# Eight modulation chunks summed by GpSimd in place of VectorE, in a one-core two-block transformer kernel

## The reference

```python
mod = jax.nn.silu(c) @ w_ada[l] + b_ada[l]            # w_ada: 1024 x 6144
sh1, sc1, gt1, sh2, sc2, gt2 = jnp.split(mod[:, None, :], 6, axis=-1)
h = modulate(rmsnorm(x, g_norm1[l]), sh1, sc1)
cq, ckv, kpe, rq, rk, rv, rg = split_proj(h @ w_in[l])
...                                                   # latent attention and retention
x_new = x + gt1 * o
x_new = x_new + gt2 * conv_ffn(modulate(rmsnorm(x_new, g_norm2[l]), sh2, sc2), ...)
```

## Time and profile before

| | |
|---|---|
| median of 3 runs | 933.84 us (929.66 to 933.9) |
| profiled execution | 929.45 us, span of its instructions 927.6 us |
| TensorE busy | 850.9 us (92%) |
| VectorE busy | 600.5 us (65%) |
| ScalarE busy | 462.0 us (50%) |
| GpSimd busy | 15.7 us (2%) |
| granted TensorE clock, mean | 0.969 of full |

### The profile page before, as it was taken

The page is one execution under the profiler, slowest core; times in us unless marked ns, Lnnn a source line. Parts: engine busy times, 40 slices in busy tenths (PEclk is TensorE's granted clock), DMA queues, the critical chain, the costliest instruction groups (busy, mean ns, idle before and its releaser), DMA issues. The chain is left out here.

```text
span 927.6 us, 13571 instructions
## 1 busy us (share of the span) xinstructions
PE 850.9 (92%) x5330; PEld 751.0 (81%) x5330; DVE 600.5 (65%) x921; ACT 462.0 (50%) x720; POOL 15.7 (2%) x21
## 2 busy tenths in 40 slices
PE   4799798989999999999999999988989699999996
PEld 2598686857889999998788967677967599999885
DVE  4956987759667888885557667466544655555443
ACT  5736255154555666664445574545444454444441
POOL 1001000000000000000000000000000000000000
PEclk9989998999899999999999999989999799999998
DMA  9932685016556556555556542234514256555541
GB/s 340 341 140 69 198 289 204 23 56 215 184 160 205 182 182 182 183 182 193 172 158 248 182 140 96 69 101 149 179 49 139 78 184 184 185 185 183 182 159 45
DMA packets 103223, 152.91 MB, mean 165 GB/s; under 512 B 6474, under 2 KB 55670, under 8 KB 103160
## 3 DMA queue, kind: packets, MB, share of 16 engines
q1 hardware_dynamic: 101160, 146.00, 48.2%
q10 hardware_dynamic: 2000, 6.04, 1.7%
HBM read 150.97 MB, written 1.05 MB: 164 GB/s over the span
## 5 line engine op out<-in xcount | busy, mean ns | idle before, releaser
L1795 DVE TENSOR_TENSOR w_lo<-raw,w_hi 128x1024 fp32r<-128x1024 f32 (+1 forms) x244 | 294.5, 1214 | 206.8 <-ACT w_hi L1306 206.6
L1306 ACT ACTIVATE w_hi<-raw 128x1024 fp32r<-128x1024 f32 (+1 forms) x244 | 254.3, 1050 | 247.6 <-PE bank L691 114.5
L765 PE MATMUL bank<-hT_hi,w_hi 128*128 128x256 f32 x864 | 246.4, 285 | 7.9 <-DVE hT_lo L1856 6.7
L766 PE MATMUL bank<-hT_lo,w_hi 128*128 128x256 f32 x864 | 245.9, 285 | 0.0
L767 PE MATMUL bank<-hT_hi,w_lo 128*128 128x256 f32 x864 | 245.8, 285 | 0.0
L765 PEld LDWEIGHTS bank<-hT_hi,w_hi 128*128 128x128 f32 x864 | 167.2, 194 | 9.3 <-issue 8.0
L767 PEld LDWEIGHTS bank<-hT_hi,w_lo 128*128 128x128 f32 x864 | 167.3, 194 | 0.0
L766 PEld LDWEIGHTS bank<-hT_lo,w_hi 128*128 128x128 f32 x864 | 167.3, 194 | 0.0
L689 PE MATMUL bank<-w_hi,hT_hi 128*128 128x512 f32 (+2 forms) x224 | 90.7, 405 | 17.4 <-DVE w_lo L1795 9.9
L690 PE MATMUL bank<-w_lo,hT_hi 128*128 128x512 f32 (+2 forms) x224 | 88.4, 394 | 0.0
L691 PE MATMUL bank<-w_hi,hT_lo 128*128 128x512 f32 (+2 forms) x224 | 88.4, 394 | 0.0
(11 more groups left out here) (317 smaller groups left out, 1172.3 us busy)
## 6 DMA issues: line engine op xcount, KB each, us to landing
raw<-w_up_dram SPq DMA_DIRECT2D x132, 256.0 KB, 3.1
raw<-w_ada_dram SPq DMA_DIRECT2D x48, 512.0 KB, 4.9
raw<-w_down_dram SPq DMA_DIRECT2D x44, 512.0 KB, 3.3
raw<-w_in_dram SPq DMA_DIRECT2D x40, 512.0 KB, 4.6
raw<-w_gate_dram SPq DMA_DIRECT2D x44, 256.0 KB, 2.8
raw<-w_out_dram SPq DMA_DIRECT2D x16, 512.0 KB, 3.6
raw<-wk_x_dram SPq DMA_DIRECT2D x8, 512.0 KB, 4.0
raw<-wv_x_dram SPq DMA_DIRECT2D x8, 512.0 KB, 3.2
```

What stands on the lines that cost most here:

```text
L765: pe.matmul(o, hi[:, c:c + P], xh[:, k, :], start=f, stop=False, skip_group_check=True)
L766: pe.matmul(o, hi[:, c:c + P], xl[:, k, :], start=False, stop=False, skip_group_check=True)
L1306: act.activation(unit_view(w_hi[n % NSPLIT], u), unit_view(raw[u % NRAW], u), ACT.Copy).then_inc(w_hi_ready, 1)
L1795: dve.tensor_tensor(unit_view(w_lo[n % NSPLIT], u), unit_view(raw[u % NRAW], u), unit_view(w_hi[n % NSPLIT], u).bitcast(F32), ALU.subtract ...
```

## The change

The 64 row tiles of the sum units are handled by GpSimd. VectorE's one fused instruction becomes two on GpSimd, since the raw tile is first multiplied in place and then added: 64 multiplications and 64 additions (four of the latter are plain copies, for the first row tile of chunks 6 to 9). Ahead of each of them GpSimd waits for its own previous instruction (`settle`). `accumulate` is called from GpSimd's loop over the norms: s0 to s15 right after the power of norm "mem", s16 to s31 right after that of "ret". `unit_ready` now counts split units only, and a new semaphore `sum_ready` counts sum units; SyncE and TensorE wait for the one that fits. VectorE skips sum units, and its feed in the rounds of "mla" is gone.

```diff
@@ TensorE @@
-                    pe.wait_ge(unit_ready, u + 1)
+                    pe.wait_ge(unit_ready, split_of[u] + 1)
...
-                pe.wait_ge(unit_ready, last_unit[f"ada{p}"] + 1)
+                pe.wait_ge(sum_ready, sum_no[last_unit[f"ada{p}"]] + 1)
@@ SyncE @@
-                    sp.wait_ge(unit_ready, u - NRAW + 1)
+                    if summed[u - NRAW]:
+                        sp.wait_ge(sum_ready, sum_no[u - NRAW] + 1)
+                    else:
+                        sp.wait_ge(unit_ready, split_of[u - NRAW] + 1)
@@ GpSimd @@
+            def accumulate(u):
+                name, k0, nk, cols, _ = units[u]
+                chunk = int(name[3:])
+                acc = sum_of(chunk)
+                pool.wait_ge(raw_landed[u % NRAW], landed[u])
+                if k0:
+                    pool.wait_ge(sum_ready, sum_no[u])
+                for k in range(k0, k0 + nk):
+                    w = raw[u % NRAW][:, (k - k0) * cols:(k - k0 + 1) * cols]
+                    settle()
+                    step(pool.tensor_scalar(w, w, csilu[:, 0, k:k + 1], None, ALU.mult))
+                    settle()
+                    if k:
+                        ins = pool.tensor_tensor(acc, acc, w, ALU.add)
+                    elif chunk in SUMMED_EARLY:
+                        pool.wait_ge(in_gate, 32)
+                        ins = pool.tensor_tensor(acc, gate_of(chunk), w, ALU.add)
+                    else:
+                        if chunk in (6, 8):
+                            for p in SUMMED_EARLY[chunk - 6:chunk - 4]:
+                                ready(pool, ("spread", p))
+                        ins = pool.tensor_copy(acc, w)
+                    if k < k0 + nk - 1:
+                        step(ins)
+                ins.then_inc(sum_ready, 1)
...
                 pool.tensor_tensor(rstd[:, n, 0:w], var[:, n, 0:w], mhalf[:, 0:w], ALU.pow).then_inc(rstd_ready, 1)
+                if name in ("mem", "ret"):
+                    pool.wait_ge(csilu_ready, 2)
+                    for u in sum_units[16 * (name == "ret"):16 * (name == "ret") + 16]:
+                        accumulate(u)
@@ VectorE: accumulate() is removed @@
                     if summed[u]:
-                        if units[u][1]:
-                            dve.wait_ge(unit_ready, u)
-                        accumulate(u)
                         continue
...
-                    elif kind == "mla":
-                        feed_units(base_unit + n + 1)
```

More of the change, by code:

```diff
@@ L282, in build @@
     split_of = {u: n for n, u in enumerate(split_units)}
+    sum_units = [u for u in range(len(units)) if summed[u]]
+    sum_no = {u: n for n, u in enumerate(sum_units)}
     ends = set(last_unit.values())
@@ L462, in build @@
         unit_ready = sem("unit_ready")
+        sum_ready = sem("sum_ready")
+        pool_step = sem("pool_step")
         w_used = sem("w_used")
@@ L1270, in _, with step, settle @@
             pool.wait_ge(mhalf_ready, 1)
+            steps = [0]
+            def step(ins):
+                steps[0] += 1
+                ins.then_inc(pool_step, 1)
+            def settle():
+                pool.wait_ge(pool_step, steps[0])
+            def accumulate(u):
[23 more added lines that the diff above has]
+                ins.then_inc(sum_ready, 1)
             for n, name in enumerate(POWS):
@@ L1758, in feed @@
                 feed_units(reach(last_unit[name] + 1 if name else 0))
[L1760 to L1782, removed]
             def feed_units(stop):
```

## The result

The changed kernel takes 996.95 us (994.28 to 998.98) against 932.65 us of the kernel before, a ratio of 1.0694 (95% interval 1.0664 to 1.0723): 64 us slower, where 8.5 had been forecast and the range ended at 958, 25 us above the kernel before. The profiled execution has a span of 997.1 us against 927.6: these two lie 69.5 us apart, because the profiled execution of the changed kernel is the slowest of its four (998.98) and that of the kernel before (929.45) lies 3 us under its median. Differences of places in the two traces add up to 69.5, not to 64.

A forecast was written before the change was run, and what follows sets the result against it. VectorE was taken to bound 95.6 to 153.9 us and TensorE attention. The terms 6.4 + 1 + 2.1 - 1 gave +8.5 us, so 942.3 us for the median, with a range of 926 to 958.

The forecast's parts named there:

- 8.5 us of idle TensorE: 95.6 to 153.9 us: the most idle TensorE time that could be won there, 58.3 less 49.8.
- P: GpSimd's time per sum unit of two row tiles, each one product and one addition of 128x512: taken as 3.9 us.
- upper bound, 6.2: Dearest GpSimd time per sum unit: two and three passes with the power's larger fixed part, 6.2 us.
- (c): Rival: GpSimd itself bounds attention, 5.0 us a unit without turns; early stretch -1, attention +19.7, total +18, 952 us; chance 0.20.
- (d): Rival: slow GpSimd and turns both, 4.5 us a unit, 6.0 with turns; +12.8, +11.7 and +1, total +25, 959 us; chance 0.10.
- turns: GpSimd and VectorE instructions locking each other out of SBUF: 1.5 us a unit in full for s4 to s15, 1.3 taken.
- Stretch 1: 78.5 to 95.6 us: GpSimd's first sums beside a busy VectorE; 0 side by side, about +9 in full turns, +6 taken.
- stretch 2: 95.6 to 153.9 us: 5.2 us a unit delays rg3's load, start 155.1 against 148.66: +6.4, the first stretch's +6 included.
- Stretch 3: 153.9 to 180.7 us: VectorE's two-tile products that TensorE waits for meet GpSimd: +1 (0 to +3).
- Attention: After power "ret": GpSimd needs 16 x 3.9 = 62.4 us, TensorE wants chunk 9 after 60.3: +2.1, no turns counted.
- (a): Rival: engines side by side without turns, 3.9 us a unit, about 8 us won early, attention +1.1; -7, 927 us; chance 0.22.
- (b): Rival: two effects cancel, 3.5 us a unit, turns as forecast; +3.2 at rg3, attention -2.7; +0.5, 934.3 us; chance 0.18.

The follow-up runs named there:

- ceiling run: Changed kernel, but GpSimd leaves the sums out and only fills the accumulator by one 128x512 memset a unit: 916.14 us against 930.31, ratio 0.9844.
- e6: Kernel before, plus 60 pairs of GpSimd scalar product and addition on unused tiles beside the first feed-forward: 953.87 us against 930.22 (+23.7).
- e7: Kernel before, plus 180 GpSimd memsets of 128x1024 on unused tiles beside the first feed-forward: 929.89 us against 930.22 (-0.3).
- e5: Changed kernel, but the product with silu(c) is written as a two-tile product instead of one with a scalar column: 974.57 us, +44.4 over the kernel before.
- e3: Changed kernel, but the product with silu(c) is left out and only the 64 additions (four copies) stay: 935.42 us, +6.5 over the kernel before.
- e10: Changed kernel, but GpSimd sums only chunks 6 and 7, with a two-tile product, VectorE the other six: 930.38 us, ratio 1.0011 to the kernel before.

## Why the prediction was wrong

**What bounds the kernel before.** Right in the main. The ceiling run shows that the early stretch gives some 12 us when VectorE's sums go. Taking the 8.5 us of idle TensorE as the most that can be won was too low: TensorE's busy time shrank too, at a clock of 1.00 in place of the 0.91 of the earlier trace rows.

**GpSimd's price, the step that failed.** P was taken as 3.9 us a unit, the mean of two prices made from a memset, which only writes, and the fixed part of a power, whose price by column (0.16 us) was left out. Measured: 6.1 alone. The addition was sized about right (1.26 against 0.95 to 1.24); the product was taken as the cheap half at 0.5 to 0.8 and is the dear one at 1.57. The upper bound, 6.2, held, but by luck: it has 1.25 for the product and 1.68 for the addition, where 1.57 and 1.26 were measured. And it was not carried into the range, which stopped at P = 5.0 and 4.5 in rivals (c) and (d). With P = 6.2 and its turns (7.5) the prediction's own sum gives 106.7 + 8 x 7.5 + 6.8 = 173.5, +24.8, for the early stretch and 16 x 6.2 - 60.3 = +38.9 for attention, together 64. That this is the difference of the medians to the microsecond is partly luck, since the terms of the trace are other ones (below). The traces lie 69.5 us apart where 8.5 had been forecast. Of the 61.0 us that were missed, 49.4 are the time of the units, 14.9 in the early stretch and 34.5 in attention: P was off by 2.2 us, times 8 and times 16, and the turns were a little less than taken. The other 11.6 are waits and turns that the sum hadn't. So the mechanism was the right one, and the step that failed is the size of P.

**The turns.** Right in kind, by e6 and e7. Stretch 1: +6 forecast, rv0 came 5.2 us late; the wait stood at rk3 (4.29) and not at rv0, where near 8 had been named. s4 was reached at 106.65, forecast 106.7, but that is luck: in the forecast GpSimd had finished s3 at 102.4 and waited for s4's load, in the trace it was still at s3 until then:

```profile
105.37 1.30 POOL L1301 TENSOR_TENSOR modrow<-modrow,raw 128x512 f32<-128x512 f32 x1
106.65 2.54 POOL L1298 TENSOR_SCALAR raw<-raw,csilu 128x512 f32<-128x512 f32 x1
```

In stretch 2 a unit cost 7.07 (s4 to s11, 106.65 to 163.2), 1.0 above its price alone; 1.3 had been taken.

**Stretch 2, the loads.** rg3 forecast at 155.1, measured at 175.22: +26.6 in place of +6.4. Of the 20.1 us, 14.9 are s11 (163.2 in place of 148.3), pace again. The other 5.2 come between s11 and rg3: its w_hi was ready at 169.6, but VectorE had the rope halves of rq and the split of cqT in front, some of them stretched by turns (1.5 in place of 0.4 us), and got to that w_lo at 173.96. That wait of 4.4 us was missing from the sum.

```profile
168.54 1.06 ACT L1354 ACTIVATE w_hi<-raw 128x1024 fp32r<-128x1024 f32 x1 [2.79 <-DMA raw<-w_in_dram]
173.96 1.21 DVE L1816 TENSOR_TENSOR w_lo<-raw,w_hi 128x1024 fp32r<-128x1024 f32 x1
```

**Stretch 3.** +1 forecast, +4.2 measured (34.7 us from rg3 to the power "ret", 30.4 before). TensorE waits 3.38 us at uq0 (185.39), where it had no wait before. The load of uq1 takes the buffer of s13, which GpSimd finished at 177.9; it landed at 181.2. ScalarE works in order, so its split of ckvT stood behind that unit, VectorE's half of it came behind ScalarE's, and uq0's w_lo behind that, at 183.22. The queue had been followed only to rg3.

```profile
183.22 4.44 DVE L1816 TENSOR_TENSOR w_lo<-raw,w_hi 128x768 fp32r<-128x768 f32 x3
```

**Attention.** +2.1 forecast, +36.6 measured: 96.8 us from the power's end to the spread of chunk 9, against 60.3. 16 x 6.1 = 97.6 is near it because two things cancel: the four copies and the borders between chunks save some 3 us, and VectorE's split of wout0 costs 2.5. That split was to give back 1 us by falling into the wait; it met GpSimd's last units instead:

```profile
292.33 1.91 POOL L1301 TENSOR_TENSOR late_sum<-late_sum,raw 128x512 f32<-128x512 f32 x1
294.39 3.41 POOL L1298 TENSOR_SCALAR raw<-raw,csilu 128x512 f32<-128x512 f32 x1 [0.16 <-issue]
```

The sum that gives P = 3.8 as the point at which it pays is borne out: at 5.0 (e5) it has 79.8 of 80 us, with chunk 7 in time and 8 and 9 late, and with additions alone (e3) nothing is late. The point itself was not tried. The part behind the last spread is 2 us longer.

**Rivals.** (a) asked for no turns and P under 4.4; both fail. (b) fails with it. (d) named both places and the sign, at well under half the size (+25); (c) had attention right in sign (+19.7) and the early stretch wrong (-1).

## What to carry to other kernels

Before work is moved to an idle engine, its price there is wanted for the very form, width and operand kinds; where no row has it, the upper bound goes through the whole sum and into the range, because a chain of 16 units multiplies it. Moved work must meet a deadline at each unit and hold no buffer that a shared load queue needs for others. And what the freed engine gains is given back in turns if the two engines read SBUF side by side: additions alone, fast enough for every deadline in attention, still cost some 20 us over the ceiling.

## What the runs showed of the hardware

A GpSimd product with one scalar takes 1.49 to 1.57 us for 128x512 float32 and is slower than an addition of two tiles (1.26), a two-tile product with a spread-out column (1.04) and a copy (0.61). A GpSimd instruction that reads SBUF lengthens VectorE's two-tile instructions (w_lo 1.22 to 1.60 us in e6), and beside it four copies of 128x128 took 2.42 us in place of 0.63 (e10); a memset does nothing of the kind (1.22 in e7). Not all two-tile instructions were hit (prod kept 0.68). Which of the two engines pays more depended on GpSimd's form: beside the same VectorE work, w_lo took 1.43 us with the scalar product and 1.77 with the two-tile one, and the quicker GpSimd made the slower kernel.
